# The second routed layer as one list of steps: 64-slot steps spread over four 128-slot experts, in alternating groups of eight pieces

## The reference, cut to what matters

```python
def moe_swiglu(x, w_router, w_gate, w_up, w_down):
    logits = (x @ w_router).astype(jnp.float32)
    top_val, top_idx = lax.top_k(logits, TOP_K)
    top_w = jax.nn.softmax(top_val, axis=-1)
    gate = jnp.einsum('bsk,bske->bse', top_w,
                      jax.nn.one_hot(top_idx, N_EXPERTS_2, dtype=jnp.float32)).astype(x.dtype)
    y = jnp.zeros_like(x)
    for e in range(N_EXPERTS_2):
        h = jax.nn.silu(x @ w_gate[e]) * (x @ w_up[e])
        y = y + gate[..., e:e + 1] * (h @ w_down[e])
    return y
```

## Time and profile before

| | us |
|---|---|
| median of three runs (2199.04 to 2201.26) | 2200.84 |
| the profiled execution | 2195.31 |
| its span, from the first to the last instruction | 2193.5 |
| TensorE busy in it | 2013.2 |
| VectorE busy | 1250.8 |
| ScalarE busy | 992.7 |

### The profile page before, as it was taken

How to read it: one execution, slowest core, us unless ns; L and a number is a source line. 1 busy time by engine, 2 the same in 40 slices (tenths; PEclk the granted TensorE clock), 3 DMA queues, 4 the chain that set the end, 5 groups by cost and what they waited for, 6 DMA issues and landing times. The chain is left out here.

```text
span 2193.5 us, 29312 instructions
## 1 busy us (share of the span) xinstructions
PE 2013.2 (92%) x11542; PEld 1499.1 (68%) x11542; DVE 1250.8 (57%) x1928; ACT 992.7 (45%) x1406; POOL 162.9 (7%) x151
## 2 busy tenths in 40 slices
PE   8997899999898889998989899999989989999896
PEld 7896885443587778997858687655655655665675
DVE  4457652222456677667276888544544545454787
ACT  3555442111244544443384668433543444344683
POOL 2103100000000003331001000000000000000000
PEclk9999998999998999999999999999999999999998
DMA  8650539999673234556603699999999999999994
GB/s 266 188 173 1 175 114 395 416 416 418 246 233 97 78 123 151 198 190 166 184 1 97 232 336 381 387 408 391 402 407 394 389 403 413 388 389 406 376 368 168
DMA packets 228362, 601.32 MB, mean 274 GB/s; under 512 B 16091, under 2 KB 121967, under 8 KB 205568
## 3 DMA queue, kind: packets, MB, share of 16 engines
q1 hardware_dynamic: 220112, 571.56, 69.7%
q0 software_dynamic: 8112, 27.91, 4.1%
HBM read 594.37 MB, written 5.05 MB: 273 GB/s over the span
## 5 line engine op out<-in xcount | busy, mean ns | idle before, releaser
L3454 DVE TENSOR_TENSOR ring_rounded<-ring,arena_rounded 128x1024 fp32r<-128x1024 f32 x268 | 313.0, 1221 | 36.6 <-ACT arena_rounded L2625 33.1
L2625 ACT ACTIVATE arena_rounded<-ring 128x1024 fp32r<-128x1024 f32 x268 | 270.8, 1059 | 52.9 <-DMA ring<-in_moe_w_down_dram 21.8
L2898 DVE TENSOR_TENSOR ring_rounded<-ring,ring_rounded 128x2048 fp32r<-128x2048 f32 (+1 forms) x68 | 147.1, 2165 | 157.0 <-ACT ring_rounded L2352 156.7
L1416 PE MATMUL psF<-ring_rounded,arena_rounded 128*128 128x512 f32 x512 | 202.6, 396 | 0.0
L2352 ACT ACTIVATE ring_rounded<-ring 128x2048 fp32r<-128x2048 f32 (+1 forms) x71 | 128.6, 1814 | 82.6 <-PE psF L1417 62.8
L1415 PE MATMUL psF<-arena_rounded 128*128 128x512 f32 x344 | 138.2, 402 | 8.6 <-ACT hT L2667 7.0
L3454 DVE TENSOR_TENSOR ring_rounded<-ring,memT_rounded 128x1024 fp32r<-128x1024 f32 x76 | 90.0, 1221 | 90.5 <-ACT memT_rounded L2625 90.2
L1417 PE MATMUL psF<-arena_rounded 128*128 128x512 f32 x344 | 136.8, 398 | 0.0
L2625 ACT ACTIVATE memT_rounded<-ring 128x1024 fp32r<-128x1024 f32 x76 | 78.2, 1060 | 89.9 <-DMA ring<-in_moe_w_down_dram 80.9
L1415 PE MATMUL psB<-yT_rounded,ring_rounded 128*128 128x256 f32 x384 | 111.1, 289 | 3.7 <-DVE ring_rounded L2898 2.8
L1416 PEld LDWEIGHTS psF<-ring_rounded,arena_rounded 128*128 128x128 f32 x512 | 97.1, 190 | 22.0
(11 more groups left out here) (589 smaller groups left out, 5009.1 us busy)
## 6 DMA issues: line engine op xcount, KB each, us to landing
ring<-in_moe_w_gate_dram SPq DMA_DIRECT2D x224, 512.0 KB, 8.2
ring<-in_moe_w_up_dram SPq DMA_DIRECT2D x224, 512.0 KB, 9.1
ring<-in_moe_w_down_dram SPq DMA_DIRECT2D x112, 1024.0 KB, 8.3
ring<-in_w_dram SPq DMA_DIRECT2D x48, 1024.0 KB, 16.3
arena<-in_w_dram SPq DMA_DIRECT2D x16, 1024.0 KB, 18.7
ring<-in_w_in_dram SPq DMA_DIRECT2D x14, 1024.0 KB, 5.5
ring<-in_ff_w_gate_dram SPq DMA_DIRECT2D x11, 1024.0 KB, 7.2
ring<-in_ff_w_up_dram SPq DMA_DIRECT2D x11, 1024.0 KB, 9.8
```

The costliest lines, as they stand in the source:

```text
L1416: mm(bank, x1, w2, start=False, stop=False, skip_group_check=open_groups)
L2625: ap_(piece(idx, w_hi).bitcast(R32), piece(idx, raw_halves), ACT.Copy).then_inc(piece_high, 1)
L2898: V.tensor_tensor(ring_r[:, slot_of[c], 0:kt * w].bitcast(R32), raw, ring_r[:, hi_slot[c], 0:kt * w], ALU.subtract).then_inc(weights_low, 1)
L3454: V.tensor_tensor(piece(idx, low_halves).bitcast(R32), piece(idx, raw_halves), piece(idx, w_hi), ALU.subtract).then_inc(piece_low, 1)
```

## The change

The steps become one list. Large steps keep their order; a small step stands behind each large step that isn't its expert's first, while there are small ones. The twelve small steps are used up with expert 5:

0.0, 0.1, 2.0, 0.2, 2.1, 0.3, 2.2, 1.0, 1.1, 2.3, 1.2, 4.0, 1.3, 4.1, 3.0, 3.1, 4.2, 3.2, 4.3, 3.3, 6.0, 5.0, 5.1, 6.1, 5.2, 6.2, 5.3, 6.3, 7.0, 7.1, 7.2, 7.3

Within a step the order of groups is now gate t, down t - 1, up t. Only where a large step is followed by another large one, or is the last (`up_first`), it stays gate, up, down. The turn of step t - 1 moves into the middle of gate t, after half its pieces. Every large step uses the banks F[0] to F[2]; its turned part goes to F[1] and F[2], or to F[3] and B[3] where a large step follows (`turn_banks`). GpSimd's list of gathers and stores is put in the new order, the marking for expert 7 comes two steps into it instead of in its first, and the lists of ScalarE and VectorE are rewritten.

```diff
-        for group in ((0,), (1, 2), (3, 4), (5, 6), (7,)):
-            for s in range(4):
-                for pos in group:
-                    self.steps.append(Step(len(self.steps), pos, s, len(group) == 1))
+        many = [(pos, s) for pos in BIG for s in range(4)]
+        few = [(pos, s) for pos in range(E2) if pos not in BIG for s in range(4)]
+        places = []
+        for pos, s in many:
+            places.append((pos, s))
+            if s and few:
+                places.append(few.pop(0))
+        self.steps = [Step(t, pos, s) for t, (pos, s) in enumerate(places)]
...
-            for part, u in (("gate", t), ("up", t), ("down", t - 1)):
+            st.up_first = st.big and (t == n - 1 or self.steps[t + 1].big)
+            down = (("down", t - 1),) if t else ()
+            parts = (("gate", t), ("up", t), *down) if st.up_first else (("gate", t), *down, ("up", t))
...
-        def many_banks(st):
-
-            return (F[3], B[2], B[3]) if st.alone and st.t % 2 else F[0:3]
+        def turn_banks(st):
+
+            followed = st.t + 1 < len(order.steps) and order.steps[st.t + 1].big
+            return (F[3], B[3]) if followed else (F[1], F[2])
...
-            for pos in (1, 2, 3, 4):
+            for pos in (2, 1, 4, 3):
                 bring_rows(pos)
```

On TensorE:

```diff
-                    if st.big and st.t == order.first_of[7] + 1:
-                        pe.wait_ge(few_y_saved, order.nth_small(n_back - 1))
-                        pe.wait_ge(last_marks_saved, 1)
...
+                def step(st, prev):
+                    if prev is None:
+                        gate(st)
+                        up(st)
+                        find_tokens()
+                        return
+                    gate(st, 0)
+                    turn(prev)
+                    if prev.last:
+                        following = [p for p in range(prev.pos + 1, E2) if (p in BIG) == prev.big]
+                        if following:
+                            turn_x(following[0])
+                    if st.t == end + 2:
+                        mark_last()
+                    gate(st, 1)
+                    if st.up_first:
+                        up(st)
+                    down(prev)
+                    if st.t == 1:
+                        turn_x(2)
+                    if not st.up_first:
+                        up(st)
```

On ScalarE:

```diff
+                    if prev is not None:
+                        turned(prev)
...
+                    if ahead:
+                        highs_of(ahead[1], ahead[0], range(4))
+                    silu(st)
+                    if st.t >= 2 and steps[st.t - 2].last:
+                        save_y(steps[st.t - 2])
+                    for part in parts:
+                        highs_of(part[1], part[0], range(4 if part == ahead or prev is None else 0, 8))
...
+                    highs_of(st.t + 1, "gate", range(8))
```

On VectorE:

```diff
+                    if not st.big:
+                        lows_of(prev.t, "down", range(8))
+                        lows_of(st.t + 1, "gate", range(4))
+                        hidden(st)
+                        lows_of(st.t + 1, "gate", range(4, 8))
+                    elif st.up_first:
+                        lows_of(st.t, "up", range(0 if prev is not None else 4, 8))
+                        lows_of(st.t - 1, "down", range(4))
+                        hidden(st)
...
+                        lows_of(st.t - 1, "down", range(4, 8))
+                        lows_of(st.t + 1, "gate", range(8))
...
+                    else:
+                        lows_of(prev.t, "down", range(8))
+                        lows_of(st.t, "up", range(8))
+                        hidden(st)
```

More of the change, by code:

```diff
@@ L2024, in sorted_layer @@
             def sorted_layer(layer):
-                steps, pick0 = order.steps, pick_r[:, 0]
+                steps, pick0, X = order.steps, pick_r[:, 0], F[0:3]
                 def big_piece(t, part, j, a=1):
@@ L2207, in sorted_layer @@
+                end, flag = order.first_of[E2 - 1], []
+                for t, st in enumerate(steps):
+                    if t == end + 1:
+                        flag.extend(crowded_flag(nc.tensor, layer))
+                    step(st, steps[t - 1] if t else None)
+                turn(steps[-1])
+                down(steps[-1])
                 for k, (t, c) in enumerate(((0, 0), (0, 1), (1, 0), (1, 1))):
@@ L2676, in sorted_layer, with step @@
                 first_sum(layer, ALPHA2, sum_started)
-                flag = []
-                for t in range(len(steps) + 1):
-                    st = steps[t] if t < len(steps) else None
-                    prev = steps[t - 1] if t else None
-                    if t == order.first_of[7] + 1:
-                        flag.extend(crowded_flag(nc.scalar, layer))
-                    if st is not None:
-                        silu(st)
+                def step(st, prev):
+                    parts = (("up", st.t), ("down", st.t - 1))[::1 if st.up_first else -1]
+                    ahead = parts[0] if steps[parts[0][1]].big and prev is not None else None
@@ L2685, in sorted_layer @@
                     if prev is not None:
                         turned(prev)
-                    if st is not None:
-                        if st.big and st.first and not st.alone or not st.big and st.last:
-                            save_x(st.pos + 1)
-                        highs_of(t, "up", range(4, 8))
-                    if t >= 2 and steps[t - 2].last and t != order.first_of[7] + 1:
-                        save_y(steps[t - 2])
-                    highs_of(t - 1, "down", range(8))
@@ L2700, in sorted_layer @@
+                flag = []
+                for t, st in enumerate(steps):
+                    if t == order.first_of[E2 - 1] + 1:
+                        flag.extend(crowded_flag(nc.scalar, layer))
+                    step(st, steps[t - 1] if t else None)
+                highs_of(len(steps) - 1, "down", range(8))
+                turned(steps[-1])
                 act.wait_ge(last_marks_saved, 1)
@@ L3553, in sorted_layer @@
-                    if t in (2, 3):
-                        (number_rows if t == 2 else gates_of_rows)()
-                    if t in (end + 2, end + 3):
-                        add_rows(t - end - 2)
-                    lows_of(t - 1, "down", range(4, 8))
-                    lows_of(t + 1, "gate", range(8))
-                    lows_of(t + 1, "up", range(4))
+                    step(st, steps[t - 1] if t else None)
+                lows_of(len(steps) - 1, "down", range(4))
+                turned(steps[-1])
```

172 lines of the change are left out of this document (76 added, 96 removed).

## The result

| | before | after |
|---|---|---|
| median of the runs on one chip | 2200.16 us (4 runs) | 2175.51 us (4 runs, 2170.62 to 2177.66) |
| ratio | | 0.9876, 95% interval 0.9859 to 0.9893 |
| the profiled execution | 2195.31 us | 2177.64 us |
| the layer in it: first product to end of the last down matmul | 1243.27 to 2175.86: 932.6 us | 1253.32 to 2158.23: 904.9 us |

The quotient of the two medians is 0.9888, inside the same interval. The forecast was 2157, in a range of 2145 to 2190. The direction and the range held, but the forecast's own, narrower range of 2145 to 2170 did not, and the time came out where the rival of the unchanged rate had put it (2176). The layer gained 27.7 us where 44.4 were forecast. The two profiled executions differ by only 17.7, since the layer began 10.05 us later in the second, though nothing ahead of it was changed. I come back to that.

What follows compares the result with a forecast made beforehand. TensorE and transfers bound the kernel in turn; alternating groups leave transfers as bound. 1997.1 + 131.4 + 3.0 = 2131.5 against 2175.9, a gain of 44.4; 2195.31 - 44.4 + 5.53 = 2156.4, said as 2157, range 2145 to 2190.

Steps and rivals of the forecast that it cites:

- the rival of the unchanged rate: Alternating large and small groups: transfers stay at 400 GB/s, the stretch takes 709.8 us, time 2176; chance 0.25.
- the alternating stretch: From expert 0's second up group to expert 7: transfers bound it, 283.9 MB at 413 GB/s, 687.4 us.
- The pauses of 3.85: Before the change, TensorE waits 3.85 us for the first large piece after three small groups.
- the low rate at the third large group: Before the change, three large groups in a row fill the ring and transfers pause: 306 GB/s.
- the 7.04: Pause near the last expert's start, on ScalarE's copy of the last small expert's output; forecast to go, 7.0 us.
- Two rivals: Every large group waits, deciding at 2.3 us each, up to 2259, chance 0.08; clock falls three times a pair, 2165.
- My own signs: 410 GB/s or more every 40 us; pairs 61 to 62 us; second up group by 1307; expert 7 near 1997.
- Start: Expert 0 to its second up group's end: TensorE-bound, ending at 1306.8; expert 2's row gather hidden, 15 us spare.
- the charges: 1 us at each of three places where a new large expert begins and two large steps adjoin, 3 us.
- 413: Rate in GB/s forecast for transfers that never starve, the mean of 415 and 411 in two 40 us stretches.
- Last expert: Expert 7, bound by TensorE: 139.9 us less 7.0 and 1.5 for two pauses gives 131.4.
- the last pause: Pause of 2.98 us after the last turn; rounding four down pieces ahead of the copy leaves half, 1.5.

Runs made afterwards that it cites:

- the shorter products: Changed kernel without the third matmul of gate and up products in experts 1, 3 and 5: 2173.0 us, layer 904.0 against 904.9.
- half the columns: Changed kernel loading small experts' pieces in their first 512 of 1024 columns, used twice, all matmuls kept: 2134.2 us, layer 866.2.
- the kernels with one part each: New step list with gate, up, down order kept: 2177.5 us; alternating groups with expert 0's four steps alone at the start: 2179.5 us.

## Why the prediction was right, and where its sizes were off

**What bounds it: right.** In the alternating stretch the transfers never stop for long, and they are the bound: shown by the shorter products (no gain) and by half the columns (38.6 us gained). The pauses of 3.85, the low rate at the third large group and the 7.04 went. Two rivals went with them: the mean pause ahead of large groups was 27.5 / 37 = 0.7 us, not 2.3, and the clock in the stretch was 0.99.

**The rival of the rate: wrong in its mechanism, right in its time.** It had the rate stay at 400 GB/s and the time at 2176. In the window from 1340 to 2010 the rate rose from 397 to 410, so this rival isn't what happened. But 2175.5 is its time and not mine, and by the time alone the two could not have been told apart. That the stated range held is in part luck: it reached to 2190 only for this rival's sake.

**My own signs: some failed.** I had asked for 410 GB/s or more in every 40 us of the alternating stretch. Of seventeen such windows from 1322 on, seven lie below, the lowest at 392 (1522 to 1562). Up group to up group, pairs took 61.5 and 60.4 us (1341.58 to 1403.12, 1920.32 to 1980.72), as forecast. The end of the second up group and the beginning of expert 7 came late, and not only by the 10.05 us of the later start; the next two parts say by how much.

**Start: 63.5 forecast, 68.6 measured, 5.1 too little.** I asked whether the gather for expert 2's rows would be in time, and it was. I didn't ask what stands behind ScalarE's copy of the turned rows on its queue: the roundings of up(0.1). With the copy moved the stretch takes 63.9, so 4.8 of the 5.1 are this place: the pause of 2.98 and the fall of the clock behind it.

**Alternating stretch: 690.3 without the charges, 703.8 measured, 13.5 too little.** The term that was off is the product of bytes and rate. The queues moved 287.85 MB in it (703.8 x 0.409) where I had 283.9, at 409 where I had 413. The rate is 287.85 / 0.409 - 287.85 / 0.413 = 6.8 us of it. The rest, 6.7, is that 4.0 MB more passed in the stretch (9.6 us) less the 2.9 that I had given for the way from the last landing to expert 7. Of the 4.0 MB, 1.0 is other traffic than weights (4.4 against 3.4). The rest are five pieces: 47 had landed at the stretch's start, where I had 49, and 587 at its end, where I had 584, three of them expert 7's.

Was 413 the wrong rate? Queued loads of gate and up landed a median of 1.28 us apart (0.524 MB, 410 GB/s) and those of down 2.49 apart (1.049 MB, 421), so a wide step of 12.58 MB takes 16 x 1.28 + 4 x 2.49 = 30.4 us, which is 413. At that pace the 540 pieces of the stretch take 685 us. Of the 19 us more, some 10 lie in the 38 intervals between landings that overlap one of GpSimd's gathers or stores (means 1.52 and 2.81). That is what their own 3.9 MB take at 409 GB/s (9.6 us), so they slow the loads by their bytes and by no more, and I had counted 3.4 MB of them. The other 9 us are spread over the rest of the intervals, and their cause stays open: 413 is the pace of a typical load, and the mean over a long stretch lies below it. In one place I was too careful: where the large experts 1, 3 and 5 begin and two large steps adjoin (1462 to 1522, 1652 to 1712 and 1832 to 1902), windows of 10 us carry 405 to 424 GB/s, so the 3 us charged for them weren't needed.

**Last expert: 131.4 forecast, 132.5 measured.** The pause of 7.04 went, as said. The estimate that 1.5 of the last pause would stay was wrong in sign: it is 3.33, more than the 2.98 before, since I looked at ScalarE's roundings and not at what VectorE has there (2.60 for the rows and two subtractions). With the addition moved it is 1.41.

**The sum.** 5.1 + 13.5 + 1.1 - 3.0 = 16.7 = 44.4 - 27.7. The medians moved by 24.7. I had taken the profiled execution of before to its median by adding 5.53; that of after lies 2.1 above its own, and the layer began 10.05 us later in it. The granted clock falls at other places in the stretch ahead of the layer from run to run; that this is all of the difference was not tested.

**A part that I had given no size of its own.** I told the gain as the alternation's. By the kernels with one part each, the list gives 9.3 us, the alternation 9.9, and 7.5 to 9.5 more at expert 7 come with either, most likely from the rewritten lists. In the sum all were there (that expert 0's last two steps no longer stand alone is in where the alternating stretch begins), but nothing in my text said that with either part alone two thirds of the gain would be there.

**The page's rate.** The Trainium skill's page "DMA: Bandwidth & Descriptors", section "Bandwidth", has about 358 GB/s for a core's loads from HBM and 425 measured with one core alone. Here 409 were sustained for 704 us and 423 for 18 us with rows of 8 KB, so the second figure is the one that this core nears.

## What to carry to other kernels

When two engines bound a stretch in turn, look at the sequence of groups within the depth of the ring, and then take away one side's work in an experiment: what stays is the other's rate. Behind every in-order instruction that is moved, list what is queued on that engine and who waits for it, also for the small copies. And take a rate from the longest stretch that is never starved: here two short windows and the median landing both gave 413 GB/s, and 704 us gave 409. Last, when a rival puts the time near your own, look for the number of the trace that parts the two; here it was the rate.

## What the runs showed of the hardware that I had not expected

- Loads into 64 of 128 rows: the core moved 291 GB/s at a full DMA share, against 410 with all rows; the same saving in columns took 38.6 us off the layer, and in rows added 70.6.
- Two rows of 4 KB per partition in one 1 MB load: 409 and 410 GB/s, no faster than one row in 512 KB. One row of 8 KB: 423 and 418.
- The pauses of 2.98 us before up(0.1) and 3.33 before the last down group were followed by 1.2 GHz over the next matmuls, the 1.41 left of the second was not, so that one cost 1.6 to 2.5 us more than itself. Elsewhere a pause of 2.02 was followed by the low level and one of 3.28 was not.
- GpSimd's gathers and stores beside saturated loads cost what their bytes cost on the whole (10 us for 3.9 MB), though one gather lowered the rate to 286 GB/s for 4 us.
- The layer's length came out at 904.9 and 904.7 in two profiled executions, while its start differed by up to 12 us between executions with the same code ahead of it.
